# Float32 rows stored, gathered and transposed once, and split into two halves behind the transpose

## What is computed

```python
def expert_choice_moe(h, w_router, w_gate, w_up, w_down):      # per request
    t = h.reshape(n_tok, D)                                    # h = rmsnorm(x, norm_ffn)
    aff = jax.nn.softmax((t @ w_router).astype(jnp.float32), axis=-1)
    gates, idx = lax.top_k(aff.T, cap)                         # 16 experts, cap = 128 and 256
    xe = t[idx]
    hid = jax.nn.silu(einsum('ecd,edf->ecf', xe, w_gate)) * einsum('ecd,edf->ecf', xe, w_up)
    ye = einsum('ecf,efd->ecd', hid, w_down) * gates[..., None]
    out = jnp.zeros((n_tok, D), h.dtype).at[idx.reshape(-1)].add(ye.reshape(-1, D))
```

## Time and profile before

| | us |
|---|---|
| median of 3 runs | 3311.46 |
| lowest and highest run | 3311.46, 3316.22 |
| profiled execution: span from the first to the last instruction | 3313.0 |
| busy in that span: PE, DVE, ACT, POOL | 2969.1, 1483.9, 1248.4, 308.5 |

### The profile page before, as it was taken

How to read it: one execution, slowest core, us unless ns; L and a number is a source line. 1 busy time by engine, 2 the same in 40 slices (tenths; PEclk the granted TensorE clock), 3 DMA queues, 4 the chain that set the end, 5 groups by cost and what they waited for, 6 DMA issues and landing times. The chain is left out here.

```text
span 3313.0 us, 44990 instructions
## 1 busy us (share of the span) xinstructions
PE 2969.1 (90%) x15831; PEld 2527.0 (76%) x15831; DVE 1483.9 (45%) x2921; ACT 1248.4 (38%) x2103; POOL 308.5 (9%) x256
## 2 busy tenths in 40 slices
PE   7999968687899799944999999999999999999990
PEld 5888867543344588834999999999999999999990
DVE  3122147365555344456454444544444444544334
ACT  3121134365566233311343443433433443433334
POOL 0000000011111000000111111111101111111100
PEclk9999988888889899966999999999999999999995
DMA  5121124233222455542455455554545544555428
GB/s 164 64 85 73 42 79 139 65 99 105 79 82 85 135 192 196 195 155 83 157 174 184 143 161 171 177 160 143 177 157 173 183 146 149 174 184 153 151 78 302
DMA packets 252956, 464.88 MB, mean 140 GB/s; under 512 B 12491, under 2 KB 97644, under 8 KB 243180
## 3 DMA queue, kind: packets, MB, share of 16 engines
q1 hardware_dynamic: 225980, 367.71, 32.0%
q0 software_dynamic: 26928, 96.55, 11.3%
HBM read 358.11 MB, written 106.10 MB: 140 GB/s over the span
## 5 line engine op out<-in xcount | busy, mean ns | idle before, releaser
L1162 DVE TENSOR_TENSOR we_lo<-we_raw,we_hi 128x1024 fp32r<-128x1024 f32 x384 | 467.4, 1225 | 626.0 <-ACT we_hi L1157 625.4
L105 PE MATMUL p_psum<-p_xT_hi,we_hi 128*128 128x384 f32 x2048 | 692.9, 338 | 0.0
L107 PE MATMUL p_psum<-p_xT_hi,we_lo 128*128 128x384 f32 x2048 | 685.3, 335 | 0.0
L106 PE MATMUL p_psum<-p_xT_lo,we_hi 128*128 128x384 f32 x2048 | 685.0, 334 | 0.0
L1157 ACT ACTIVATE we_hi<-we_raw 128x1024 fp32r<-128x1024 f32 x384 | 400.0, 1051 | 6.0 <-DMA we_raw<-w_gate 5.8
L106 PEld LDWEIGHTS p_psum<-p_xT_lo,we_hi 128*128 128x128 f32 x2048 | 384.7, 188 | 0.6
L105 PEld LDWEIGHTS p_psum<-p_xT_hi,we_hi 128*128 128x128 f32 x2048 | 384.3, 188 | 0.6
L107 PEld LDWEIGHTS p_psum<-p_xT_hi,we_lo 128*128 128x128 f32 x2048 | 384.4, 188 | 0.0
L105 PE MATMUL p_psum<-we_hi,p_hid_hi 128*128 128x512 f32 x768 | 300.0, 391 | 0.0
L107 PE MATMUL p_psum<-we_hi,p_hid_lo 128*128 128x512 f32 x768 | 299.0, 389 | 0.0
L106 PE MATMUL p_psum<-we_lo,p_hid_hi 128*128 128x512 f32 x768 | 298.9, 389 | 0.0
(11 more groups left out here) (213 smaller groups left out, 4610.8 us busy)
## 6 DMA issues: line engine op xcount, KB each, us to landing
we_raw<-w_gate SPq DMA_DIRECT2D x32, 2048.0 KB, 7.7
we_raw<-w_up SPq DMA_DIRECT2D x32, 2048.0 KB, 8.0
we_raw<-w_down SPq DMA_DIRECT2D x32, 2048.0 KB, 8.5
h<-p_h_split SPq DMA_DIRECT2D x24, 1024.0 KB, 3.9
zT<-p_z SPq DMA_DIRECT2D x54, 256.0 KB, 2.0
p_x<-x POOLq DMA_DIRECT2D x6, 2048.0 KB, 8.3
p_q_raw<-zT SPq DMA_DIRECT2D x96, 128.0 KB
p_m_raw<-mixT SPq DMA_DIRECT2D x24, 512.0 KB, 5.0
```

Source lines behind the costliest of these rows:

```text
L105: pe.matmul(out, lhi, rhi, start=first, stop=False)
L106: pe.matmul(out, lhi, rlo, start=False, stop=False)
L107: return pe.matmul(out, llo, rhi, start=False, stop=last)
L1162: dve.tensor_tensor(self.lo[:, n % self.HL, ks], self.raw[:, n % self.RAW, ks], self.hi[:, n % self.HL, ks].bitcast(F32), ALU.subtract).th ...
```

## The change

The normalised row is stored once, as float32, straight from `h2_sb`, so that `h2` has 1024 numbers per token, not 2048; ACT's copy and DVE's subtraction in `mixer_out` go. A wait is added there: DVE may write `h2_sb` only when the store from it, two tiles ago, has landed. In `experts` the gather brings 1024 float32 numbers per row, PE transposes eight steps of three pieces with float32 operands (source, identity and result), ACT copies each bank to `xT_hi`, and DVE subtracts `xT_hi` from the same bank to get `xT_lo`, so that DVE now waits for ACT. Each bank is used once, and only `x_lo_done` frees it. The load of the identity goes from POOL's queue to SP's.

```diff
@@ mixer_out
-        h2_split = sb("h2_split", [P, 2, 2 * D], F32R)
-        h2_v = h2.bitcast(F32).rearrange("(t p) d -> t p d", p=P)
+        h2_v = h2.rearrange("(t p) d -> t p d", p=P)
...
-                sp.wait_ge(h2_lo_done, t)
-                sp.dma_start(h2_v[t - 1], h2_split[:, 1 - b].bitcast(F32)).then_inc(h2_stored[1 - b], 16)
+                sp.wait_ge(h2_done, t)
+                sp.dma_start(h2_v[t - 1], h2_sb[:, 1 - b]).then_inc(h2_stored[1 - b], 16)
...
-                if 1 <= lags <= 2:
-                    if not isinstance(t, int) or t >= 3:
-                        act.wait_ge(h2_stored[o], turn_value(t - 1, o, 16) - 16)
-                    act.wait_ge(h2_done, t)
-                    act.activation(h2_split[:, o, :D], h2_sb[:, o], ACT.Copy).then_inc(h2_hi_done, 1)
...
                     if not isinstance(t, int) or t >= 3:
                         dve.wait_ge(t_mm, t - 2)
+                        dve.wait_ge(h2_stored[o], turn_value(t - 1, o, 16) - 16)
                     dve.scalar_tensor_tensor(out=h2_sb[:, o], in0=x2_sb[:, o], scalar=rstd[:, o:o + 1], in1=gain[:, :],
                                              op0=ALU.mult, op1=ALU.mult).then_inc(h2_done, 1)
...
-                if 1 <= lags <= 2:
-                    dve.wait_ge(h2_hi_done, t)
-                    dve.tensor_tensor(h2_split[:, o, D:], h2_sb[:, o], h2_split[:, o, :D].bitcast(F32), ALU.subtract).then_inc(h2_lo_done, 1)
@@ experts
-        xe = sb("xe", [P, ST, 2 * D], F32R)
+        xe = sb("xe", [P, ST, D])
-        ident_r = sb("ident", [P, P], F32R)
+        ident = sb("ident", [P, P])
...
+            sp.dma_start(ident[:, :], ident_d).then_inc(ident_in, 16)
...
-            pool.dma_start(ident_r[:, :], ident_d.bitcast(F32R)).then_inc(ident_in, 16)
             gather(0)
...
-                    act.wait_ge(t_mm, e * (2 * KT) + 2 * k + 1)
-                    act.activation(xT_hi[:, k], ps[:, 2 * k % 8, :SLOTS], ACT.Copy).then_inc(x_hi_done, 1)
+                    act.wait_ge(t_mm, e * KT + k + 1)
+                    act.activation(xT_hi[:, k], ps[:, k, :SLOTS], ACT.Copy).then_inc(x_hi_done, 1)
...
-                    dve.wait_ge(t_mm, e * (2 * KT) + 2 * k + 2)
-                    dve.tensor_copy(xT_lo[:, k], ps[:, (2 * k + 1) % 8, :SLOTS]).then_inc(x_lo_done, 1)
+                    dve.wait_ge(x_hi_done, e * KT + k + 1)
+                    dve.tensor_tensor(xT_lo[:, k], ps[:, k, :SLOTS], xT_hi[:, k].bitcast(F32), ALU.subtract).then_inc(x_lo_done, 1)
...
-                for i in range(2 * KT):
-                    bank, k = i % 8, i // 2
-                    if i >= 8:
-                        rows_read(e, bank, 0)
-                    elif first and bank == 7:
+                for k in range(KT):
+                    if first and k == 7:
                         pe.wait_ge(list_read, 1)
                     elif not first:
-                        used = sg_done if bank < 4 else hid_done
-                        pe.wait_ge(used, e * (2 * FT) - FT + bank % 4 + 1)
+                        used = sg_done if k < 4 else hid_done
+                        pe.wait_ge(used, e * (2 * FT) - FT + k % 4 + 1)
                     for st in range(ST):
-                        source = xe[:, st, (i % 2) * D + k * P:(i % 2) * D + (k + 1) * P]
-                        last = pe.transpose(ps[:, bank, st * P:(st + 1) * P].bitcast(F32R), source, ident_r[:, :])
+                        last = pe.transpose(ps[:, k, st * P:(st + 1) * P], xe[:, st, k * P:(k + 1) * P], ident[:, :])
                     last.then_inc(t_mm, 1)
 
-            def rows_read(e, bank, turn):
+            def rows_read(e, bank):
 
-                pe.wait_ge((x_hi_done, x_lo_done)[bank % 2], e * KT + turn * (KT // 2) + bank // 2 + 1)
+                pe.wait_ge(x_lo_done, e * KT + bank + 1)
@@ build
-    h2 = nc.dram_tensor("h2", (NT, 2 * D), F32R, kind="Internal").ap()
+    h2 = internal("h2", NT, D)
```

More of the change, by code:

```diff
@@ L949, in mixer_out @@
         lg = sb("lg", [P, TT, NE])
-        const_in, h2_hi_done, h2_lo_done = (sem(n) for n in ("const_in", "h2_hi_done", "h2_lo_done"))
+        const_in = sem("const_in")
         m_in, x_in, x2_stored, h2_stored = ([sem(f"{n}{i}") for i in range(2)] for n in ("m_in", "x_in", "x2_stored", "h2_stored"))
@@ L1425, in gather @@
             def gather(e):
-                listed, transposed = held(pool, turn[0], e * 2 + 2), held(pool, turn[1], e * (2 * KT))
+                listed, transposed = held(pool, turn[0], e * 2 + 2), held(pool, turn[1], e * KT)
                 pool.wait_ge(list_done, 2)
@@ L1629, in expert @@
                             pe.wait_ge(y_done[0], e * ST)
-                            rows_read(e, 0, 1)
                         elif n == 1 and j == 0:
@@ L1642, in expert @@
                             if n == 0 and j == 0:
-                                pe.wait_ge(x_hi_done, e * KT + k + 1)
                                 pe.wait_ge(x_lo_done, e * KT + k + 1)
@@ L1656, in expert @@
                         if more:
-                            rows_read(e + 1, 4 * half + st, 1)
+                            rows_read(e + 1, 4 * half + st)
                         else:
```

## The result

The changed kernel takes 3291.88 us (median of five runs, 3285.94 to 3297.14), the kernel before 3311.46 on the same chip (3305.21 to 3316.22): a ratio of 0.9933, 95% interval 0.9916 to 0.9951. The change is faster, as forecast, but by 19.6 us and not by 28.7, and 3291.88 lies 0.9 above the top of the range (3291). The profiled executions have spans of 3291.0 and 3313.0.

What follows compares the result with a forecast made beforehand. PE was taken to bound the expert loop and mixer_out. Gains of 23.0 (fifteen blocks), 5.0 (first gather) and 0.7 (first block) make 28.7 us: 3313.0 to 3284.3, less 1.5 for the median, 3282.8; range 3277 to 3291.

Steps and rivals of the forecast that it cites:

- Fifteen blocks, 23.0 us: Expert loop: 24 float32 transposes in place of 48 float32r, 2.57 us a block against 4.10; 23.0 us gained (21.5 to 26.0).
- What is late next: Behind the loop's transposes: ACT's copies and DVE's subtractions end after PE's transposes, but PE doesn't have to wait; no cost.
- First gather, 5.0 us (2.0 to 5.6): First expert: with half the bytes the gather's third part lands 5.0 us sooner, between 2.0 and 5.6.
- the identity load which leaves POOL's queue moves nothing: First gather: POOL idles 9.33 us for the list anyway, so moving the identity load to SP's queue changes nothing.
- a gather landing as late as before: Named sign of being wrong, at the first expert; if right, its transposes would start near 1541 us.
- First block, 0.7 (-1.0 to 1.5): First expert's transposes, at 1.2 GHz after idling: 5.1 us against 5.80, 0.7 gained; 1.0 lost to 1.5 gained.
- mixer_out at nothing: ACT's 24 copies and DVE's 24 subtractions lie beside PE's products; removing them gains nothing (54 us if on PE's path).
- Sum: Whole program: 23.0 + 5.0 + 0.7 = 28.7 us gained, with ends of 22.5 and 33.1.
- dearer transposes: Rival, experts: a float32 transpose takes twice as long as elsewhere; 17.4 us slower, 3329; loses from 0.171 us each; chance 0.04.
- a period held by another chain: Rival, expert loop: scatter to next split weights sets the period, blocks give nothing, 5.7 us left, 3305.8; chance 0.05.
- a wait for DVE: Rival, expert loop: PE waits for DVE's last subtraction, about 5.2 us after the block's start; 3322 us; chance 0.02.
- The rival of PE waiting for the chain: Expert loop: PE waits for ACT's copies then DVE's subtractions, losing 2.6 us a turn; 3322 us; chance 0.02.

Runs made afterwards that it cites:

- the first pair of profiles: Profiles from the first comparison, the changed kernel and the kernel before on one chip: 3291.88 us against 3311.46, ratio 0.9933.
- the second (5.85 to 4.78): Second profiles of the kernel before and of the changed kernel, neither edited: 3319.05 us before, 3292.03 changed (one run).
- the third run of the changed kernel: The changed kernel, unedited, timed once more on another chip against the kernel before: 3289.19 us against 3315.54, ratio 0.9924.

## Why the prediction was right, and where it was off

- *Fifteen blocks, 23.0 us:* right. 22.99 measured; a block takes 2.54 where 2.57 was taken from other stages' float32 transposes. That it agrees to 0.01 is luck: the 4.10 taken for a block before is also 0.02 above the mean of the fifteen, 4.08, and the two errors cancel.
- *What is late next:* right. ACT's and DVE's copies end 1.6 and 2.8 us after PE has begun the down products, and PE doesn't wait.
- *First gather, 5.0 us (2.0 to 5.6):* the step that failed; 0.9 came, below the lower end. Two things went into it. First, "the identity load which leaves POOL's queue moves nothing" is wrong: without that load the first gather's issue takes 1.9 us in place of 1.16, the third part is issued 1.15 later after the list, and PE waits about 1.6 us longer. The argument looked at when the load was done and not at what it did to POOL's queue. Second, the bytes' share was over-sized: half the gather was put at 3.9 "if the gather had it to itself", and "sharing makes it more". With the bytes alone changed the gain is 3.4, less than 3.9, and holding the weight chunk back gives another 2.6 of idle time: the chunk takes its share, as the lower end had assumed. 3.4 - 1.6 leaves 1.8, and the rest of the way to 0.9 is the part whose cause isn't shown above. The sign of being wrong that was named, "a gather landing as late as before", nearly came: PE's first transpose is at 1548.48, not near 1541, and only 0.9 us sooner after the list than before.
- *First block, 0.7 (-1.0 to 1.5):* 1.84 in the first pair of profiles, above the upper end, and 1.07 in the second (5.85 to 4.78); the block takes 4.55 in the third run of the changed kernel. The forecast had the low clock for all 24 transposes. In the changed kernel's first profile the granted clock rose within them; when it does differs between executions.
- *mixer_out at nothing:* right, shown by putting the copies back.
- *Sum:* 28.7 forecast against 25 from the list on: the gather gave 4.1 less than forecast, and in the first pair the first block 1.1 more, which hides a part of it. The first comparison's 19.6 has the varying time before the list in it, 3.2 us in the profiled pair, which the range had allowed for with too little: one kernel's list alone moves by 11.6 us from execution to execution. Where the comparisons of whole programs landed, at 19.6, 27.0 and 26.4, is therefore in part chance.
- *Rivals:* dearer transposes (0.109, threshold 0.171), a period held by another chain, and a wait for DVE all fall. The rival of PE waiting for the chain was priced at 2.6 us a turn; forced, it costs 4.0 on average: 3.1 for the wait, as the chain is longer than estimated, and 0.9 because in nine of 15 turns the granted clock is low behind it.

The windows of PE's first block of transposes in the changed kernel, with the busy time (count), the granted clock, the DMA share and GB/s, show that rise:

```profile
1548.00:1550.00 2.00, 1.52 (x8) 0.50 0.78 287
1550.00:1552.00 2.00, 2.00 (x14) 0.66 0.00 1
1552.00:1554.00 2.00, 0.68 (x7) 1.00 0.00 0
```

## What to carry to other kernels

Where PE is busy throughout, count what the change takes off PE's stream, in durations of that very form from elsewhere in the trace; work taken from other engines and from DMAs counts only where PE waits, as at the first expert. A load that is moved off a queue which has long been idle can have been doing something there besides its bytes: look at what then comes first on that queue. For small changes, compare from a common event behind the part that varies between executions, not whole programs.

## What the runs showed of the hardware that was not expected

- POOL's first gather, with no DMA of POOL's in the 438 us before it, takes 1.9 us to issue; with a load of four columns 9.3 us ahead of it, it takes 1.16, and that load's own issue takes 0.57. Why, the runs don't show, nor whether it is the idling or being first in the stage that matters; the second gather's issue takes 1.9 with and without such a load.
- A wait of 2.87 us on PE behind 24 transposes, in a loop in which it is else busy all the time, is followed in nine of 15 turns by a stretch near the lower clock, for about 3.7 us at 0.53 in the turn shown: 4.0 us lost per turn on average, where the wait alone makes 3.1.
- The first expert's slowest gather part lands 11.3 us after its issue with rows of 8 KB beside 2.1 MB of weights (the kernel with wide rows), after 7.9 with rows of 4 KB, and after 5.9 with those and the weights held back.
